# Where the halves of the outputs and the score maxima stand in the queues of a sliding-window attention

## The reference

```python
def odd_mixer(h, w_in, b_in, w_out, b_out, sinks, cos_r, sin_r):
    proj = h @ w_in + b_in
    q, k, v = jnp.split(proj, [C_Q_WIDTH, C_Q_WIDTH + C_KV_WIDTH], axis=-1)
    q = apply_rope(split_heads(q, C_Q_HEADS, C_HEAD_DIM), cos_r, sin_r)
    k = apply_rope(split_heads(k, C_KV_HEADS, C_HEAD_DIM), cos_r, sin_r)
    y = sliding_window_sink_attention(q, k, v, sinks)
    return merge_heads(y) @ w_out + b_out
```

## Time and profile before

| | us |
|---|---|
| median of three runs | 2217.91 |
| lowest and highest | 2217.45, 2218.46 |
| profiled execution | 2217.45 |
| its span | 2215.7 |
| TensorE busy | 2136.4 (96%) |
| VectorE busy | 1620.9 (73%) |
| ScalarE busy | 986.0 (45%) |

### The profile page before, as it was taken

One profiled execution on the slowest core, in us unless ns is written; L12 is line 12 of the kernel. 1 busy time (PEld: TensorE's weight loads), 2 busy tenths in 40 slices (PEclk: granted clock), 3 DMA queues, 4 the chain that ended last, 5 costly groups with the idle time before them and its releaser, 6 DMA issues.

```text
span 2215.7 us, 25961 instructions
## 1 busy us (share of the span) xinstructions
PE 2136.4 (96%) x9844; PEld 1755.8 (79%) x9844; DVE 1620.9 (73%) x1681; ACT 986.0 (45%) x1312; POOL 9.4 (0%) x21
## 2 busy tenths in 40 slices
PE   4799999999999999999999999999999999999998
PEld 3678878878888888888887877778888888888886
DVE  6999888988788988777667676687665545455546
ACT  4354444454443344434445456464444344434444
POOL 0000000000000000000000000000000000000000
PEclk9899999999999999999999999999999999999999
DMA  9978779859889999977755633458765555555543
GB/s 397 421 317 311 303 307 373 344 239 361 336 323 369 376 388 378 375 288 288 281 210 232 213 129 119 143 197 322 283 247 199 193 190 189 188 191 190 190 152 152
DMA packets 82557, 593.02 MB, mean 268 GB/s; under 512 B 9424, under 2 KB 9584, under 8 KB 10912
## 3 DMA queue, kind: packets, MB, share of 16 engines
q1 hardware_dynamic: 81216, 587.31, 69.2%
q0 software_dynamic: 1248, 4.44, 0.7%
HBM read 589.62 MB, written 2.10 MB: 267 GB/s over the span
## 4 chain that ended last, share of the span: by engine, by line
PE 83%; DVE 9%; DMA 3%; ACT 3%; DVEq 1%; issue 1%; SPq 0%; ACTq 0%
PE ps L1405 26%; PE ps L1407 26%; PE ps L1406 26%; DVE w_lo L830 3%; DMA ada_raw<-in_ada 2%; PE ps L1393 2%; DVE ada_raw L834 2%; DMA raw<-in_ab_in 1%; PE ps L1433 1%; PE ps L1435 1%; PE ps L1434 1%; ACT w_hi L490 1%; ACT gate L594 1%; DVE gate L834 0%; DVE spare L834 0%
## 5 line engine op out<-in xcount | busy, mean ns | idle before, releaser
L830 DVE TENSOR_TENSOR w_lo<-raw,w_hi 128x1024 fp32r<-128x1024 f32 x728 | 880.8, 1223 | 431.9 <-ACT w_hi L490 427.6
L490 ACT ACTIVATE w_hi<-raw 128x1024 fp32r<-128x1024 f32 x728 | 764.0, 1060 | 948.7 <-PE ps L1407 772.4
L1405 PE MATMUL ps<-w_hi,xT_hi 128*128 128x512 f32 x1940 | 768.7, 396 | 28.9 <-DVE xT_lo L1108 25.6
L1407 PE MATMUL ps<-w_hi,xT_lo 128*128 128x512 f32 x1940 | 759.9, 392 | 0.0
L1406 PE MATMUL ps<-w_lo,xT_hi 128*128 128x512 f32 x1940 | 759.5, 392 | 0.0
L1405 PEld LDWEIGHTS ps<-w_hi,xT_hi 128*128 128x128 f32 x1940 | 366.6, 189 | 109.9 <-DVE xT_lo L1108 27.9
L1407 PEld LDWEIGHTS ps<-w_hi,xT_lo 128*128 128x128 f32 x1940 | 366.8, 189 | 78.0
L1406 PEld LDWEIGHTS ps<-w_lo,xT_hi 128*128 128x128 f32 x1940 | 367.4, 189 | 74.1
L834 DVE SCALAR_TENSOR_TENSOR ada_raw<-ada_raw,cond 128x2048 f32<-128x2048 f32 x176 | 402.0, 2284 | 10.0 <-DMA ada_raw<-in_ada 8.3
L1405 PE MATMUL ps<-w_hi,hT_hi 128*128 128x512 f32 x896 | 351.5, 392 | 0.0
L1407 PE MATMUL ps<-w_hi,hT_lo 128*128 128x512 f32 x896 | 348.9, 389 | 0.0
(11 more groups left out here) (185 smaller groups left out, 879.5 us busy)
## 6 DMA issues: line engine op xcount, KB each, us to landing
ada_raw<-in_ada SPq DMA_DIRECT2D x176, 1024.0 KB, 6.8
raw<-in_ffn_in SPq DMA_DIRECT2D x176, 1024.0 KB, 5.0
raw<-in_ffn_out SPq DMA_DIRECT2D x88, 1024.0 KB, 5.0
raw<-in_ab_in SPq DMA_DIRECT2D x48, 1024.0 KB, 9.0
raw<-in_swa_in SPq DMA_DIRECT2D x20, 1024.0 KB, 4.9
raw<-in_ab_out SPq DMA_DIRECT2D x16, 1024.0 KB, 7.9
raw<-in_swa_out SPq DMA_DIRECT2D x16, 1024.0 KB, 4.9
spare<-in_ada SPq DMA_DIRECT2D x8, 1024.0 KB, 9.0
```

The source lines that it names most:

```text
L490: nc.scalar.activation(w_hi[:, p % PAIRS, :, :], raw[:, t % RAW, 2 * (p % 2):2 * (p % 2) + 2, :], ACT.Copy).then_inc(hi_ready, 1)
L830: tt(w_lo[:, p % PAIRS, :, :], raw[:, (p // 2) % RAW, 2 * (p % 2):2 * (p % 2) + 2, :], w_hi[:, p % PAIRS, :, :].bitcast(F32), ALU.subtract ...
L1405: mm(out, hi[:, kt, tok], w_hi[:, q % PAIRS, k, :], start=(kt == 2 * ps0), stop=False)
L1407: last = mm(out, lo[:, kt, tok], w_hi[:, q % PAIRS, k, :], start=False, stop=(kt == 2 * ps1 - 1))
```

## The change

Three moves in the queues of ACT and DVE; TensorE's, GpSimd's and SyncE's queues stay as they are, and so does each instruction.
- On ACT, the high half of the outputs (line 794) goes from base+10, behind that step's high half, to base+9, ahead of that step's high half. That is step s+1 of the next unit, so it stands directly behind the exponentials of that unit (at step 49 for the last). The scaling goes from behind the high half of step s+1 to ahead of it. The new order is: exponentials w, half of the outputs w-1, scaling w, high half of step s+1.
- On DVE, the residue (line 1330) goes from step s+2 of the next unit, behind low half and evacuation, to step s+1 of it, behind `c_recip`'s scaling and ahead of the low half.
- On DVE, the maxima go from behind the low half of step s to ahead of it, and with them, for units 1 and 3, the last copy of transposes, which stands at the same step.

```diff
-C_ACT = {4: "exps", 5: "scale", 7: "copy0", 8: "copy2", 10: "hi"}
-C_DVE = {4: "tops", 7: "copy1", 8: "copy3", 10: "lo"}
-C_RECIP = 5
+C_ACT = {4: "exps", 7: "copy0", 8: "copy2"}
+C_DVE = {7: "copy1"}
+C_TOPS, C_RECIP, C_HALVES = 4, 5, 9
@@ scalar engine
+            def c_early(g):
+
+                for w in range(C_UNITS):
+                    if g == c_base(w) + C_HALVES:
+                        act.wait_ge(yT_done, 4 + w + 1)
+                        nc.scalar.activation(hT_hi[:, 2 * w:2 * w + 2, :], yT_c, ACT.Copy).then_inc(yTh_done, 1)
+                    if g == c_base(w) + C_RECIP:
+                        pr = probs_c[w % 2]
+                        act.wait_ge(rden_done, w + 1)
...
+                        last.then_inc(scaled_act, 1)
             for c in range(4):
                 for p in range(8):
+                    c_early(8 * c + p)
                     hi(C_Q, c, p)
                     c_stages(8 * c + p)
             for n in range(32):
+                c_early(32 + n)
                 hi(C_OUT, 0, n)
                 c_stages(32 + n)
@@ vector engine
+            def c_residue(w):
+
+                dve.wait_ge(yTh_done, 4 + w + 1)
+                tt(hT_lo[:, 2 * w:2 * w + 2, :], yT_c, hT_hi[:, 2 * w:2 * w + 2, :].bitcast(F32),
+                   ALU.subtract).then_inc(yTl_done, 1)
-            def c_recip(g):
+            def c_early(g):
 
                 for w in range(C_UNITS):
+                    if g == c_base(w) + C_TOPS:
+                        if w - 1 in C_BEHIND:
+                            copy_pT(probs_c[(w - 1) % 2][:, 3, :], heads_before(3 + w, "C") + 4, 2)
+                        tops(4 + w, 64 ** -0.5, c_at=4 * w)
                     if g == c_base(w) + C_RECIP:
...
                         last.then_inc(scaled_dve, 1)
+                        if w:
+                            c_residue(w - 1)
+                if g == c_base(C_UNITS - 1) + C_HALVES:
+                    c_residue(C_UNITS - 1)
```

More of the change, by code:

```diff
@@ L772, in _ @@
                 hi(C_KV, 0, p)
+            def c_early(g):
[6 more added lines that the diff above has]
+                        act.wait_ge(rden_done, w + 1)
+                        for t in range(TT):
+                            for e in range(2):
+                                part = pr[:, 2 * e, 128 * t:128 + 256 * t]
+                                last = nc.scalar.activation(part, part, ACT.Copy, scale=rden[:, 0, t, 2 * e:2 * e + 1])
+                        last.then_inc(scaled_act, 1)
             def c_stages(g):
@@ L780, in c_stages @@
                         exps(u, 64 ** -0.5, pr, c=True)
[L781 to L787, removed]
                     if stage == "copy0":
@@ L791, in c_stages @@
                         copy_pT(pr[:, 1, :], heads_before(u, "C") + 3, 3)
-                    if stage == "hi":
-                        act.wait_ge(yT_done, u + 1)
-                        nc.scalar.activation(hT_hi[:, 2 * w:2 * w + 2, :], yT_c, ACT.Copy).then_inc(yTh_done, 1)
                 if g == 11:
@@ L1321, in c_stages @@
                     pr, ahead = probs_c[w % 2], w not in C_BEHIND
-                    if stage == "tops":
-                        tops(u, 64 ** -0.5, c_at=4 * w)
                     if stage == "copy1":
                         copy_pT(pr[:, 2, :], heads_before(u, "C") + 2, 7)
[L1326 to L1331, removed]
+                        if ahead:
+                            copy_pT(pr[:, 3, :], heads_before(u, "C") + 4, 2)
                 for c in range(4):
@@ L1345, in _ @@
                 for p in range(8):
-                    c_recip(8 * c + p)
+                    c_early(8 * c + p)
                     lo(C_Q, c, p)
@@ L1369, in _ @@
             for n in range(32):
-                c_recip(32 + n)
+                c_early(32 + n)
                 lo(C_OUT, 0, n)
```

## The result

| | kernel before | changed kernel |
|---|---|---|
| median, us | 2217.45 (7 runs) | 2225.3 (7 runs) |
| lowest and highest | 2216.1, 2218.64 | 2220.61, 2228.82 |
| profiled execution | 2217.45 | 2223.17 |
| its span | 2215.7 | 2221.4 |

The ratio is 1.0034, 95% interval 1.0024 to 1.0044. The prediction was +2.5 us, 2220.4, with a range up to 2223.4. The change costs more, and its times spread over 8 us where those before spread over 2.5. Both need an explanation.

The account below looks back on a forecast made before the run. TensorE, busy 96% of the span, was taken as the bound, with at most 11.1 us of gaps to win. Shifts at its gates summed to +2.5 us on the median 2217.91, giving 2220.4, with an 8-in-10 range of 2216.2 to 2223.4.

Parts of the forecast that it names:

- The evacuation takes the residue's place: At pairs 16, 24, 32, 36, 40, 44 and 48, TensorE waits on the evacuations instead, 1.3 to 2.8 us each, about 13 in all.
- The sum of the queues: Shifts of TensorE's place in the second attention, added gate by gate from unit 0 to pair 48: +2.5 us.
- (a): ACT's outputs' half waits for the output matmuls with everything behind it; pair s can start at H + 6.72, or H + 6.54.
- (b): Residue behind DVE's own scaling: TensorE's 9.3 us of waits on it go, and the evacuation is late next.
- (c): Score maxima ahead of the low half of step s: 1.14 us earlier in units 1, 3, 5, elsewhere 0 to 0.1.
- (d): Restart of TensorE on a semaphore ahead of a pair costs 0.14 us; no other queue moves.
- H: Start of ACT's copy of the outputs' half: later end of exponentials or output matmuls, plus 0.04 us.
- (C): Rival: gaps at pairs 36, 40 and 44 each bring a clock dip of 1.7 us, 5.1 in all: 2225.5 us; chance 0.04.
- The term for the norm: Clock dip in this layer's last norm may be missing or longer after the shift: -1.7 to +1.7 us.
- (A): Rival: residue waits go and nothing takes their place, 2208.6 us, or 2213 for half of it; chance 0.08.
- (B): Rival: ACT's wait for the outputs feeds itself, eight chains 0.35 us longer each, 2224.0 us; chance 0.11.
- (D): Rival: gains and losses of the change cancel within 0.5 us, 2217.9 us; chance 0.12.

## Why the prediction was wrong, point by point

**What bounds the kernel.** Right: only TensorE's gaps count, and a shift at pair 48 reaches the end in full (behind that layer's last norm the changed kernel has one wait of TensorE, 0.2 us; from pair 48 to the end it takes 791.24 us, the kernel before 791.16).

**The evacuation takes the residue's place.** Right, at all seven pairs named, and for the reason given. The waits are 1.56, 1.55, 1.56, 1.74, 1.74, 2.49 and 0.67 us, 11.3 in all; I had said about 13, and for pair 48 at least 1.3. One reading behind it had its sign turned: in the earlier trace rows the evacuation ends at 1389.15 + 1.23 = 1390.38, 0.09 behind the recorded start of the residue and not ahead of it. The sum does not use this number.

**The sum of the queues.** Right within 0.06 us at each gate up to unit 5, and in total: +2.37 measured with the clock kept up, +2.5 predicted. (a), (b), (c) and (d) stand: of the chains from H to the pair that the rows give, 6.54 and 6.72, the changed kernel has 6.51 (units 2 and 4) and 6.70, 6.69, 6.70 (units 5, 6, 7). The split by parts agrees roughly: on TensorE's way to pair 48 the maxima alone take -2.3 us and the halves alone +4.1 without falls, +1.8 together.

**The clock.** This is the step that failed. The prediction took the granted clock of 1.00 in the earlier trace rows as the clock of the changed kernel's attention too, and gave rival (C) 4 chances in 100, with the argument that one gap of 2.7 us had passed without a fall. That was one gap in one execution, beside five of 1.4 to 1.9; the change makes six stretches of 3.4 us or more without a weight matmul where one was. In its place the runs show falls of 1.6 us each, three in one execution and six in the other, 4.8 and 9.5 us that the sum had at nothing.

And the same trace had an example at hand. The earlier trace rows was read as a dip after a few us in which TensorE mostly stood. TensorE before that dip, which starts at 1473.5:

```profile
1468.54 1.48 PE L1393 MATMUL ps<-ident,work 128*128 128x128 f32 x12
1470.26 0.66 PE L1393 MATMUL ps<-ident,work 128*128 128x128 f32 x4 [0.24 <-DVE x L902]
1472.70 2.98 PE L1393 MATMUL ps<-ident,work 128*128 128x128 f32 x16 [1.79 <-DVE work L890]
```

It stood for 2.0 of those 5 us and transposed for most of the rest: a gap of 1.79 beside transposes, like the gaps that the change makes.

The size that (C) was given was about right: three falls of 1.7 each on top of the forecast gave 2225.5, measured 2225.3. That the two are so close is partly luck: how many falls the median execution had is not known, and another one had six. The rule of the Trainium skill cited there (TensorE: Matmul & The Clock Gate, Why this matters for your kernels), that idle gaps between matmuls cost the clock, is borne out here in its direction. Where it differs the measurement decides: it names idle gaps longer than any of these, and in the changed kernel's two profiles gaps of 1.55 to 2.49 us behind transposes were followed by a fall at nine gates of twelve.

**The range.** It reached 1.9 us too short. It took in one fall more or less at the norm, and none in the attention; had (C) been given a weight, it would have reached 2225.5. The term for the norm, -1.7 to +1.7, was mis-sized as well: from pair 48 to the end the eight profiles with a fall there take 791.0 to 791.6 us and the five without 791.1 to 791.2, so it costs 0.5 at most.

**The other rivals.** (A) fell: all seven pairs wait. (B) fell: no chain from H is longer than the rows made it, and unit 1 gave back its 0.85. The sign that I had set for (B), a wait of the outputs' half of more than 1.5 us, came at the last unit (5.78 us; the others have 0.16 to 1.30), and it says nothing for (B): ACT comes early there, and the chain behind it took 5.31 us from H, against 5.30 by the sum. (D) fell: the measured change is 7.9 us.

## What to carry to other kernels

Before an operation is moved ahead because somebody waits for it, look what ends just before it and stands behind it in the new order: here the evacuation ended 0.6 us ahead of the residue's end, so freeing the residue could not win the 9.3 us of waits that named it until the evacuation moved too. A wait set in the middle of an engine's queue is paid by everything behind it: the 1.3 us that ACT stood reached TensorE as a gap ahead of a pair, through the scaling, two high halves, two low halves and the evacuation. And where the bounding engine idles again and again, count a fall of its clock in at a real chance: in the two profiles of the changed kernel it made 7.2 and 11.9 us out of 2.4 us of waits, and it was kept off by work that computes nothing.

## What was not expected of the hardware

The clock's fall differs between executions of the same program with the same gaps: three in one, six in another, 1.6 us each, and the times, which spread over 2.5 us before, spread over 8. And matmuls that nobody needs, 1.4 us of them in a gap of 1.7, took all falls away and made the kernel 6.6 us faster.
